# Thirteen dense projections of a two-block model: three fp32r products for each f32 product, or one f32 product

## The reference

```python
p = h @ w_in                                   # both blocks; latent tokens, and context tokens for some columns
x = x + m_lat[2] * (mix @ w_out)               # first block
y = sigmoid(g_ssd) * (y_ssd @ w_o_ssd) + sigmoid(g_att) * (y_att @ w_o_att)
x = x + gate * (y @ w_out)                     # second block
x = x + gate * (ffn(h @ w_up) @ w_down)
```

## Time and profile before

| | |
|---|---|
| median of the runs | 4677.69 us (4676.04 to 4678.01) |
| profiled execution: span from the first to the last instruction | 4676.2 us |
| TensorE busy | 3468.8 us (74%) |
| VectorE busy | 2909.6 us (62%) |
| ScalarE busy | 1528.0 us (33%) |
| GpSimd busy | 1362.9 us (29%) |
| mean granted TensorE clock | 0.878 of full speed |

### The profile page before, as it was taken

The page is one execution under the profiler, slowest core; times in us unless marked ns, Lnnn a source line. Parts: engine busy times, 40 slices in busy tenths (PEclk is TensorE's granted clock), DMA queues, the critical chain, the costliest instruction groups (busy, mean ns, idle before and its releaser), DMA issues. The chain is left out here.

```text
span 4676.2 us, 54928 instructions
## 1 busy us (share of the span) xinstructions
PE 3468.8 (74%) x18716; PEld 2774.4 (59%) x18716; DVE 2909.6 (62%) x4362; ACT 1528.0 (33%) x1968; POOL 1362.9 (29%) x512
## 2 busy tenths in 40 slices
PE   6683767876777777777777676877676987877968
PEld 3473537865565666666656345757355865766856
DVE  5224647773799998999999645349747823144441
ACT  5110421112355555555555431112013521212121
POOL 0020000001255555655555202115320033333423
PEclk9895888967899999999999888887788998988989
DMA  6110000000587887887887531000010022222322
GB/s 250 50 61 9 5 25 1 1 15 23 214 296 270 299 295 273 297 294 273 298 296 281 190 117 50 35 26 1 0 45 7 1 72 72 73 71 77 98 66 74
DMA packets 136745, 573.07 MB, mean 123 GB/s; under 512 B 12977, under 2 KB 17457, under 8 KB 103729
## 3 DMA queue, kind: packets, MB, share of 16 engines
q1 hardware_dynamic: 136528, 570.21, 34.4%
HBM read 568.07 MB, written 2.10 MB: 122 GB/s over the span
## 5 line engine op out<-in xcount | busy, mean ns | idle before, releaser
L1841 POOL TENSOR_TENSOR ex_d_low<-ex_d,ex_d_high 128x1024 fp32r<-128x1024 f32 x256 | 800.3, 3126 | 724.8 <-ACT ex_d_high L1823 724.8
L1770 PE MATMUL psum<-ex_gu_high,ex_xe 128*128 128x256 f32 x2048 | 560.0, 308 | 371.6 <-DVE ex_gu_low L1876 367.3
L1770 PEld LDWEIGHTS psum<-ex_gu_high,ex_xe 128*128 128x128 f32 x2048 | 417.2, 204 | 497.5 <-DVE ex_gu_low L1876 424.2
L1876 DVE TENSOR_TENSOR ex_gu_low<-ex_gu,ex_gu_high 128x2048 fp32r<-128x2048 f32 x256 | 620.5, 2424 | 63.0 <-ACT ex_gu_high L1812 51.3
L1770 PE MATMUL psum<-ex_gu_low,ex_xe 128*128 128x256 f32 x2048 | 535.0, 295 | 0.0
L1812 ACT CAST ex_gu_high<-ex_gu 128x2048 fp32r<-128x2048 f32 x256 | 486.7, 1901 | 9.7 <-DMA ex_gu<-in_w_gate_up 5.8
L1770 PEld LDWEIGHTS psum<-ex_gu_low,ex_xe 128*128 128x128 f32 x2048 | 418.7, 204 | 0.9
L1892 DVE CAST ex_hT<-ex_hid 128x64 fp32r<-128x64 f32 x256 | 400.8, 1565 | 8.9
L466 POOL TENSOR_TENSOR out_w_low<-out_w,out_w_high 128x1024 fp32r<-128x1024 f32 x16 | 39.3, 2463 | 786.6 <-ACT out_w_high L431 786.6
L1823 ACT CAST ex_d_high<-ex_d 128x1024 fp32r<-128x1024 f32 x256 | 266.1, 1040 | 2.7 <-PE psum L1794 2.4
L1794 PE MATMUL psum<-ex_d_high,ex_hT 128*128 128x512 f32 x512 | 229.7, 449 | 12.4 <-POOL ex_d_low L1841 9.8
(11 more groups left out here) (552 smaller groups left out, 8331.0 us busy)
## 6 DMA issues: line engine op xcount, KB each, us to landing
ex_gu<-in_w_gate_up SPq DMA_DIRECT2D x256, 1024.0 KB, 6.6
ex_d<-in_w_down SPq DMA_DIRECT2D x256, 512.0 KB, 5.7
mod_w<-in_w_mod SPq DMA_DIRECT2D x24, 2048.0 KB, 9.2
ff_up_w<-in_w_up SPq DMA_DIRECT2D x44, 512.0 KB, 3.5
ff_down_w<-in_w_down SPq DMA_DIRECT2D x16, 704.0 KB, 4.0
out_w<-in_w_out SPq DMA_DIRECT2D x16, 512.0 KB, 3.4
in2x_w<-in_w_in_x SPq DMA_DIRECT2D x16, 512.0 KB, 3.2
in2z_w<-in_w_in_z SPq DMA_DIRECT2D x16, 512.0 KB, 3.3
```

The source lines that it names most:

```text
L1770: ins = pe.matmul(k.bank(c % 2, 2 * P), xe[:, (c // NCH) % 2, t, :, :].rearrange("p a c -> p (a c)"), w, start=t == 0 and p_ == 0, stop=t ...
L1841: pool.tensor_tensor(dw_lo[:, q % 2, :], dw[:, b, :], dw_hi[:, q % 2, :], ALU.subtract).then_inc(s["down_low"], 1)
L1876: v.tensor_tensor(gu_lo[:, c % 2, :, :], gu[:, b, :, :], gu_hi[:, c % 2, :, :], ALU.subtract).then_inc(s["up_low"], 1)
```

## The change

`project` is rewritten. It has one product for each step, f32 by f32, with the weight tile as it was loaded and x as it is; all high and low halves are gone, and with them the work of ScalarE, VectorE and GpSimd that made them. The loops over tiles are written out. The weight tiles lie in a ring of up to six buffers (four in `ff_down`), each a whole tile, so that SP issues up to six loads at the start of a stage; the sums lie in a ring of eight PSUM slots of one bank or four of two. The callers lose `split`, `pieces` and register indices; their arithmetic is otherwise the same.

```diff
-def project(k, name, w, kt, tiles, unroll, x, streams, out_of, readers="vector", split=None, pieces=1, buffers=None, more=()):
+def project(k, name, kt, x, jobs, readers="vector", buffers=6):
...
+    width = max(len(streams) for _, _, streams, _ in jobs)
+    slots = 8 // width
+    tiles = [(w, i, streams, out_of) for w, tiles, streams, out_of in jobs for i in range(tiles)]
+    buffers = min(buffers, len(tiles))
...
             @block.sync
             def _(sp):
...
+                for n, (w, i, _, _) in enumerate(tiles):
+                    if n >= buffers:
+                        sp.wait_ge(summed, n - buffers + 1)
+                    sp.dma_start(wbuf[n % buffers][:, :, :], w[i, :, :, :]).then_inc(loaded[n % buffers], 16)
 
             @block.tensor
             def _(pe):
...
-                    if split:
-                        pe.wait_ge(w_low[b], n + 2)
-                        parts = ((whi[b], split[1]), (whi[b], split[2]), (wlo[b], split[1]))
...
+                for n, (_, _, streams, _) in enumerate(tiles):
+                    pe.wait_ge(loaded[n % buffers], 16 * (n // buffers) + 16)
+                    if n >= slots:
+                        pe.wait_ge(taken, n - slots + 1)
                     for s, (rhs, _) in enumerate(streams):
...
+                        for t in range(kt):
+                            ins = pe.matmul(banks(n, streams)[s], wbuf[n % buffers][:, t, :], rhs(x, t),
+                                            start=t == 0, stop=t == kt - 1)
+                    ins.then_inc(summed, 1)
...
             def reader(eng):
...
+                for n, (_, i, streams, out_of) in enumerate(tiles):
+                    eng.wait_ge(summed, n + 1)
+                    out_of(eng, i, banks(n, streams)).then_inc(taken, 1)
...
-                if split:
-                    for t in range(0, kt, 2):
-                        act.copy(split[1][:, t, :], split[0][:, t, :]).then_inc(x_high[0], 1)
...
-                        v.tensor_tensor(split[2][:, t, :], split[0][:, t, :], split[1][:, t, :],
-                                        ALU.subtract).then_inc(x_low, 1)
...
-                            pool.tensor_tensor(wlo[b][:, :, :], wbuf[b][:, :, :], whi[b][:, :, :],
-                                               ALU.subtract).then_inc(w_low[b], 1)
...
-        project(k, "ff_down", d["w_down_2"], FT_, KT, 2, a, [(ALL, S)], add, split=parts_of(k, "ff_a", a, tmp),
-                pieces=2, buffers=2)
...
+        project(k, "ff_down", FT_, a, [(d["w_down_2"], KT, [(ALL, S)], add)], buffers=4)
```

More of the change, by code:

```diff
@@ L68, in __call__ @@
         self.eng.wait_ge(self.sem, self.n)
[L71 to L80, removed]
 class Core:
@@ L384, in _ @@
             @block.tensor
             def _(pe):
[L386 to L389, removed]
-                        pe.wait_ge(w_low[b], n + 2)
-                        parts = ((whi[b], split[1]), (whi[b], split[2]), (wlo[b], split[1]))
[L392 to L396, removed]
-                    for s, (rhs, _) in enumerate(streams):
[L398 to L412, removed]
-            def reader(eng):
[L415 to L422, removed]
@@ L470, in parts_of @@
-def parts_of(k, name, x, ctx):
-    return x, *(k.sb(f"{name}_{part}", list(x.shape), ctx, mybir.dt.float32r) for part in ("high", "low"))
 ALL = lambda x, t: x[:, t, :]
@@ L655, in _, with q_out, out @@
                     v.tensor_copy(tm[:, t, 512:W], k.bank(2 * (t % 4) + 1, W - 512)).then_inc(copied, 1)
-    def q_out(eng, i, u, banks):
-        return eng.tensor_copy(qf[:, bass.ds(i * 2 + u, 1), :].rearrange("p a n -> p (a n)"), banks[0])
+    def q_out(eng, i, banks):
+        return eng.tensor_copy(qf[:, i, :], banks[0])
     def k_out(to):
-        def out(eng, i, u, banks):
-            eng.tensor_copy(to[:, bass.ds(i * 2 + u, 1), 0:L].rearrange("p a n -> p (a n)"), banks[0])
-            return eng.tensor_copy(to[:, bass.ds(i * 2 + u, 1), L:T].rearrange("p a n -> p (a n)"), banks[1])
+        def out(eng, i, banks):
+            eng.tensor_copy(to[:, i, 0:L], banks[0])
+            return eng.tensor_copy(to[:, i, L:T], banks[1])
         return out
     both = [(OF_CTX, L), (OF_LAT, S)]
-    with ExitStack() as tmp:
-        project(k, "in1", d["w_in_q"], KT, 6, 2, h, both[1:], q_out, split=parts_of(k, "h1", h, tmp),
-                more=[(d["w_in_k"], 4, both, k_out(kf)), (d["w_in_c"], 6, both, k_out(kc))])
+    project(k, "in1", KT, h, [(d["w_in_q"], 6, both[1:], q_out), (d["w_in_k"], 4, both, k_out(kf)),
+                              (d["w_in_c"], 6, both, k_out(kc))])
 def pad_heads(k, name, jobs, zeroed):
@@ L2026, in window_attention, with q_out, k_out @@
         qT = k.sb("at_qT", [P, KT, S], tmp)
-        with ExitStack() as own:
-            def q_out(eng, i, u, banks):
-                return eng.tensor_copy(qT[:, bass.ds(i * 2 + u, 1), :].rearrange("p a n -> p (a n)"), banks[0])
-            def k_out(eng, i, u, banks):
-                eng.tensor_copy(kT[:, bass.ds(i * 2 + u, 1), 0:L].rearrange("p a n -> p (a n)"), banks[0])
-                return eng.tensor_copy(kT[:, bass.ds(i * 2 + u, 1), L:T].rearrange("p a n -> p (a n)"), banks[1])
-            project(k, "in2qk", d["w_in_q2"], KT, 8, 2, h, [(OF_LAT, S)], q_out, split=parts_of(k, "at_h", h, own),
-                    more=[(d["w_in_k2"], 2, [(OF_CTX, L), (OF_LAT, S)], k_out)])
+        def q_out(eng, i, banks):
+            return eng.tensor_copy(qT[:, i, :], banks[0])
+        def k_out(eng, i, banks):
+            eng.tensor_copy(kT[:, i, 0:L], banks[0])
+            return eng.tensor_copy(kT[:, i, L:T], banks[1])
+        project(k, "in2qk", KT, h, [(d["w_in_q2"], 8, [(OF_LAT, S)], q_out),
+                                    (d["w_in_k2"], 2, [(OF_CTX, L), (OF_LAT, S)], k_out)])
         qz = k.sb("at_qz", [P, HEADS, S], tmp)
@@ L2066, in window_attention, with convolved @@
                              for f in range(KT) for t in range(ST)])
-def convolved(k, name, w, tiles, first, h, y, split=None):
+def convolved(k, name, w, tiles, first, h, y):
     step = k.sem(f"{name}_conv_step")
@@ L2408, in gate_output, with z_out @@
         rstd = k.sb("go_rstd", [P, S], tmp)
-        def z_out(eng, i, u, banks):
-            return eng.activation(z[:, bass.ds(i * 2 + u, 1), :].rearrange("p a n -> p (a n)"), banks[0], ACT.Silu)
-        with ExitStack() as own:
-            lat = h[:, :, L:T]
-            project(k, "in2z", d["w_in_z2"], KT, FT, 2, lat, [(ALL, S)], z_out, readers="scalar",
-                    split=parts_of(k, "z_h", lat, own))
+        def z_out(eng, i, banks):
+            return eng.activation(z[:, i, :], banks[0], ACT.Silu)
+        project(k, "in2z", KT, h, [(d["w_in_z2"], FT, [(OF_LAT, S)], z_out)], readers="scalar")
         with nc.Block() as block:
@@ L2450, in merge @@
     step = k.sem("mg_step")
-    flat = lambda x: x.rearrange("p a n -> p (a n)")
     with ExitStack() as tmp:
         merged = k.sb("mg_merged", [P, KT, S], tmp)
-        chain = {}
-        def ssd_out(eng, i, u, banks):
-            return eng.tensor_copy(flat(merged[:, bass.ds(i * 2 + u, 1), :]), banks[0])
-        def gate_out(eng, i, u, banks):
-            return eng.activation(flat(gates[:, bass.ds(i * 2 + u, 1), :]), banks[0], ACT.Sigmoid)
-        def att_out(eng, i, u, banks):
-            if u == 0:
-                chain["step"] = LoopSteps(eng, step, i, 2 * 2)
-            to = flat(merged[:, bass.ds(i * 2 + u, 1), :])
-            of_ssd, of_att = (flat(gates[:, bass.ds(i * 2 + u + b * KT, 1), :]) for b in range(2))
-            ins = eng.tensor_tensor(of_att, banks[0], of_att, ALU.mult)
-            chain["step"](eng.tensor_tensor(to, to, of_ssd, ALU.mult))
-            chain["step"](eng.tensor_tensor(to, to, of_att, ALU.add))
-            return eng.nop()
-        def add(eng, i, u, banks):
-            x = flat(k.x[:, bass.ds(i * 2 + u, 1), :])
-            return eng.scalar_tensor_tensor(x, banks[0], k.mod2[:, bass.ds(i * 2 + u + 16, 1), 0], x, ALU.mult, ALU.add)
-        with ExitStack() as own:
-            project(k, "o_ssd", d["w_o_ssd"], D_SSD // P, KT, 2, yT, [(ALL, S)], ssd_out,
-                    split=parts_of(k, "o_ssd", yT, own), pieces=2, buffers=2)
-        gates = k.sb("mg_gates", [P, 2 * KT, S], tmp)
-        with ExitStack() as own:
-            lat = h[:, :, L:T]
-            project(k, "in2g", d["w_in_g2"], KT, 2 * KT, 2, lat, [(ALL, S)], gate_out, readers="scalar",
-                    split=parts_of(k, "gate_h", lat, own))
-        for name, w, x, out in (("o_att", d["w_o_att"], attT, att_out), ("out2", d["w_out_2"], merged, add)):
-            with ExitStack() as own:
-                project(k, name, w, KT, KT, 2, x, [(ALL, S)], out, split=parts_of(k, name, x, own))
@@ new lines, in merge, with ssd_out, gate_out, att_out @@
+        chain = Steps(k.nc.vector, step)
+        def ssd_out(eng, i, banks):
+            return eng.tensor_copy(merged[:, i, :], banks[0])
```

(15 more changed lines are left out.)

119 lines of the change are left out of this document (29 added, 90 removed).

## The result

The changed kernel takes 4831.72 us (median of 4 runs, 4830.55 to 4836.1) against 4677.85 us for the kernel before (4 runs). The ratio is 1.0332, with a 95% interval from 1.0318 to 1.0346. Forecast were 4828 us and a range from 4805 to 4852. The profiled execution has a span of 4828.8 us, 152.6 more than before; its own time is 4831.03 us, 2.2 above the span.

The account below looks back on a forecast made before the run. The prediction took TensorE's own pace as the bound between a projection's first and last product. 4676.2 + 263.4 (windows) - 113.2 (openings) = 4826.4; with the span 1.5 us under the runs' median, 4828 us, range 4805 to 4852.

Parts of the forecast that it names:

- The pace of TensorE: In twelve projections' windows, an f32 step takes 0.858 us against 0.680 for three fp32r products: 263.4 us more.
- The rival of four times 0.227 a step: In every f32 step, four passes at the fp32r pace, 0.907 instead of 0.858 us: 4904 us, chance 0.03.
- the faster one (4514): In each of 1664 steps, the second f32 instruction costs no more than one fp32r product, 0.656 us: 4514, chance 0.02.
- The start of each window: Each stage's window has 1.8 us for start and end, mostly lower clock after idling; range -19 to +12 us over twelve.
- The openings: From each stage's first load to first product, splitting x and the weight goes away: 113.2 us less over twelve stages.
- Edits costed at nothing: Changes to loads, readers and loops in the projections, each taken as 0 us in the sum.
- Six loads at once: At stage start, the queue serves the first load first: 0 us; upper bound some 1 us a stage, +12.
- later loads: Within a window, 512 KB per 6.9 us is less than ff_up now moves per 5.44: ample cover, 0 us.
- readers: VectorE's work in ff_up is 2.3 us a tile against TensorE's 6.9; with eight banks it cannot stop TensorE: 0 us.
- written-out loops: In each stage, taken as 0 us; register work saved up to -4 over twelve, longer program up to +6.
- The rivals of shared loads (4948): At stage openings, six tiles landing together take 13 us instead of 3.4: +120, 4948 us, chance 0.04.
- a starved TensorE (4861): In the written-out code, instruction supply stalls TensorE, say 0.02 us a step over 1664 steps: +33, 4861 us, chance 0.05.

Follow-up runs that it names:

- The products ahead of the first one: Changed kernel with four f32 products of 256 columns on constants ahead of each projection's first product: 4802.25 us, ratio to the kernel before 1.0270.
- the kernel with loops: Kernel before with one edit, no operands split, so each step is one f32 product, still in loops with two weight buffers: 4832.32 us, ratio 1.0331.

## Why the prediction was right, and what in it was not

**The pace of TensorE: right.** Two f32 instructions of 0.429 us against three fp32r ones of 0.227 were forecast from the earlier trace rows; `ff_up` came out at 304.2 where 303.9 was worked out, the two `in2x` at 84.4 and 85.1 where 84.35 was. Windows +272.9 instead of +263.4, and nearly all of the difference is the next term. The Trainium skill, page "FP8 and Floating Point Precision", section "TensorE Precision Notes", has true FP32 at four passes; the ratio of the measured paces, 3.8 passes of fp32r to a step, agrees with it in kind. The rival of four times 0.227 a step (4904 us) is ruled out by the window of `ff_up`, which it would have put at 321, and so is the faster one (4514): no window is shorter than its steps at 0.858.

**The start of each window: mechanism right, size too small.** This is the term of 1.8 us a stage taken from `in2bc`. The thirteen windows exceed 1414.9 (the steps alone, 1440 by 0.858, 224 by 0.432 and 82.6 for `in2bc`) by 33.2, which is 2.6 a stage. In `in2z` the first seven instructions started 0.85 us and more apart, and its window came out at 113.2 instead of 111.6. The products ahead of the first one showed that it is the clock: windows at 1.00 lose it. What the text reckoned with, from the shorter idle time ahead of a stage, is that the change would shorten this loss to 1.8 us each. It did not: what the granted clock lacks to 1.00, by each window's length and summed over the thirteen, is 30.8 us before and 29.8 after. Half as much idle time ahead of a stage (5.7 us instead of 12.2 in `in2g`) bought nothing here, and `in2bc`, the one stage taken as the measure, was among those that lost least.

**The openings: sum right, cause wrong.** -109.0 instead of -113.2. The difference is mostly late first loads (4.8 in `in2x0`, 4.7 in `in2g`, 4.5 in `out1`, where 3.4 was taken); `o_ssd` had 5.9 for 5.6 and `ff_down` 6.3 for 7.0. But the text said that the time ahead of the first product goes to "splitting x, then the weight, on VectorE and GpSimd one behind the other". That holds for `in2z` and `in2g` alone. In the other ten the free-bank signal of line 416 stood behind the split, and 47 us of the kernel's time could have been had without any change of the product, as the kernel with the bank signal moved ahead of the split shows. I read the releaser of `in2g`, the one kind of stage where it is GpSimd, and took it for all. The forecast did not suffer, since the change removes both causes.

**Edits costed at nothing: right in sum, but for the edges.** Six loads at once, later loads, readers and written-out loops moved nothing in all: with loops and two buffers the time was the same. The rivals of shared loads (4948) and of a starved TensorE (4861) are out, the first by openings of 3.3 to 3.7 us in eight stages, the second by the window of `ff_up` at its steps. The edges gave back 11.3 us; the text allowed 4 in the range and took 0. A part of it, 0.4 to 0.7 us where projections follow each other, comes with the loops written out, as the kernel with loops shows; that it is register work was argued and not shown. The rest lies in the long stretches of other stages, and one trace of each kernel doesn't tell it from chance.

**The sum.** +272.9 - 109.0 - 11.3 = +152.6, against +263.4 - 113.2 = +150.2. Errors of +9.5, +4.2 and -11.3 nearly cancel: that the forecast came within 4 us of the time is in part luck, for it was better than its terms.

## What to carry to other kernels

Before trading several cheap products for one exact one, read the number and pitch of TensorE's instructions for both forms; where TensorE is the bound, dropping the work that it hides on other engines is worth nothing, however many microseconds it adds up to. An opening and a pace are separate terms: the slow form may be right for the first tile, while the fast one's operands are being made. A signal that a buffer is free belongs ahead of everything else in its engine's queue, or better, isn't needed on first use; the releaser column names it, and each kind of stage has to be looked at.

## What the runs showed that I had not expected

Short idle times cost clock. The changed kernel's windows stand some 2.6 us a stage above their steps, for instructions at the lower clock level (0.85 us from one start to the next instead of 0.43 with 512 columns). `in2g` is one of these stages, though TensorE sat idle for only 5.7 us ahead of it and had been at the higher level until 4 us into that idle time. Eight instructions on constants in between, with 1.05 us of idle time ahead of them in `in2g` and 1.4 behind, kept the granted clock at 1.00 there; 29.5 us for 104 added instructions.

Six loads of 512 KB in the queue of the `in2x` stages instead of two moved the median landing from 3.3 to 5.8 us and not the first one: it came after 4.8 and 3.3 us there, against 5.6 and 3.3 with two. A 16 KB packet of an instruction queue under way together with the first load goes with 1 to 2 us more in the opening. The eight written-out kernels met it in 0 to 5 of their thirteen stages (12 in all), the three with loops in none.
